# PEER experts: 16 more tokens take gathered rows instead of dense columns, and half the low parts are made on GpSimd

## What is computed

```
sc, pos = lax.top_k(cand, PEER_TOPK)
idx = jnp.take_along_axis(cidx, pos, axis=-1)
gate = jax.nn.softmax(sc, axis=-1)
ug = jnp.take(u_tab, idx, axis=0)
act = jax.nn.gelu(jnp.einsum('td,thkd->thk', xb, ug).astype(jnp.float32), approximate=False)
vg = jnp.take(v_tab, idx, axis=0)
return jnp.einsum('thk,thkd->td', (gate * act).astype(xb.dtype), vg)
```

## Time and profile before

| | us |
|---|---|
| three runs | 3080.49, 3080.64, 3084.59 |
| median | 3080.64 |
| profiled execution, its own time as its span | 3083.4 |
| first stage, first matmul to start of the second | 608.4 to 1303.4 |
| second stage | 1303.4 to 1840 |

### The profile page before, as it was taken

One profiled execution on the slowest core, in us unless ns is written; L12 is line 12 of the kernel. 1 busy time (PEld: TensorE's weight loads), 2 busy tenths in 40 slices (PEclk: granted clock), 3 DMA queues, 4 the chain that ended last, 5 costly groups with the idle time before them and its releaser, 6 DMA issues. The chain is left out here.

```text
span 3083.4 us, 55647 instructions
## 1 busy us (share of the span) xinstructions
PE 3001.1 (97%) x20151; PEld 2650.7 (86%) x20151; DVE 2225.1 (72%) x3952; ACT 981.6 (32%) x1828; POOL 1124.6 (36%) x806
## 2 busy tenths in 40 slices
PE   9999989899999999999999999999999999899999
PEld 7688868799999999999999997768888878688887
DVE  8766687798898898688888887677775345577741
ACT  3444430334433334333333333561111023321110
POOL 4234235222122222243333334214555443345553
PEclk9999999999999999999999999999999999899999
DMA  4000032377877878899999953112223241123233
GB/s 171 28 3 3 3 113 78 131 241 254 299 247 263 286 251 268 297 388 359 352 348 340 354 202 105 33 55 89 96 99 92 79 99 35 58 88 99 98 92 93
DMA packets 242033, 507.91 MB, mean 165 GB/s; under 512 B 44566, under 2 KB 135846, under 8 KB 238412
## 3 DMA queue, kind: packets, MB, share of 16 engines
q1 hardware_dynamic: 183116, 321.11, 31.0%
q0 software_dynamic: 36864, 134.23, 13.4%
q10 hardware_dynamic: 21888, 50.34, 4.2%
HBM read 453.17 MB, written 52.44 MB: 164 GB/s over the span
## 5 line engine op out<-in xcount | busy, mean ns | idle before, releaser
L202 POOL TENSOR_TENSOR up_low<-normed,up_high 128x1024 fp32r<-128x1024 f32 (+1 forms) x136 | 317.0, 2331 | 299.9 <-DVE up_high L197 299.9
L3147 POOL DMA_INDIRECT ev_rows<-in_v,ev_list x128 | 177.3, 1385 | 326.5 <-DVE ev_row_sum L3214 313.6
L207 PE MATMUL up_ps<-ffn_high,up_high 128*128 128x512 f32 x704 | 274.9, 390 | 3.0 <-DVEq L833 3.0
L209 PE MATMUL up_ps<-ffn_high,up_low 128*128 128x512 f32 x704 | 273.9, 389 | 0.0
L208 PE MATMUL up_ps<-ffn_low,up_high 128*128 128x512 f32 x704 | 273.9, 389 | 0.0
L207 PE MATMUL eu_ps<-norm_unit_high,expert_high 128*128 128x384 f32 x768 | 265.7, 346 | 0.0
L209 PE MATMUL eu_ps<-norm_unit_high,expert_low 128*128 128x384 f32 x768 | 258.2, 336 | 0.0
L208 PE MATMUL eu_ps<-norm_unit_low,expert_high 128*128 128x384 f32 x768 | 257.9, 336 | 0.0
L197 DVE CAST up_high<-normed 128x1024 fp32r<-128x1024 f32 (+1 forms) x136 | 92.5, 680 | 205.4 <-PE up_down_ps L209 150.6
L2823 POOL DMA_INDIRECT expert_scores<-in_u,eu_list x64 | 84.0, 1313 | 268.3 <-DVE eu_dots L2851 260.0
L3172 ACT ACTIVATE expert_high<-mixed 128x1024 fp32r<-128x1024 f32 x95 | 100.8, 1061 | 229.3 <-PE ev_acc L209 212.9
(11 more groups left out here) (721 smaller groups left out, 8633.5 us busy)
## 6 DMA issues: line engine op xcount, KB each, us to landing
mixed<-in_v SPq DMA_DIRECT2D x128, 512.0 KB
normed<-in_u SPq DMA_DIRECT2D x125, 512.0 KB
normed<-in_w_up SPq DMA_DIRECT2D x88, 512.0 KB, 3.4
expert_act<-mixed ACTq DMA_DIRECT2D x128, 192.0 KB
expert_gates<-eu_gates ACTq DMA_DIRECT2D x24, 1024.0 KB
expert_scores<-expert_gates SPq DMA_DIRECT2D x16, 1536.0 KB
normed<-expert_act SPq DMA_DIRECT2D x128, 192.0 KB
normed<-in_w_down SPq DMA_DIRECT2D x32, 448.0 KB, 3.3
```

What stands on the lines that cost most here:

```text
L202: return nc.gpsimd.tensor_tensor(low.bitcast(F32R), of, high, ALU.subtract)
L207: nc.tensor.matmul(out, w_high.bitcast(F32R), x_high.bitcast(F32R), start=start, stop=False)
L209: return nc.tensor.matmul(out, w_low.bitcast(F32R), x_high.bitcast(F32R), start=False, stop=stop)
L3147: nc.gpsimd.indirect_dma_start(rows[:, b % 4, :], None, v, bass.IndirectOffsetOnAxis(ap=list_[:, b % 8:b % 8 + 1], axis=0)).then_inc(fetch ...
```

## The change

1. `DENSE` goes from 384 to 368. The last 16 tokens of group 3 take gathered rows too. Their 16 x 128 experts are spread over the 128 partitions, 8 partitions to a token and 16 columns each, so that one gather serves 8 experts of each of the 16 tokens: 16 gathers from each table. Their numbers and gates get into that form through HBM, by two small stores and two loads on SP after tile 33.
2. Group 3 is now chosen first, then 1 and 2. The gate phase of the first round is written out, without the gate matmuls of 2 of its 16 tiles.
3. First stage: VectorE makes only the first half of each low part. For the second half ScalarE copies the PSUM bank once more into SBUF (two places, `copied`), and GpSimd subtracts. GpSimd's program per tile is the low part of tile b+3, then the gather of tile b+3, and from tile 32 on, in every even tile, one more gather (`fetch_more`) into one place, `more.row`: 16 from `u_tab` for the 16 tokens, then 32 from `v_tab` for group 0. VectorE meets it in the odd tile (`meet_more`): a dot, or a weighed sum into `more.sum`.
4. Second stage: 96 + 16 adds instead of 128, in seven of every eight tiles, with seven row places instead of four. At the end eight small matmuls (`together`) sum up the 16 tokens' partitions.
5. The place for all this is the residual `c.x`. It is stored to HBM (2 MB) at the start of `peer_scores` on SP, and loaded again at the end of the second stage.
6. In the memory stage ScalarE spreads the 16 tokens over 128 columns, TensorE turns them by 8 transposes ahead of the first key product, and ScalarE copies the result; the value products wait for that. Semaphores are also cleared at the start of the first stage, on GpSimd.

The core of the diff:

```diff
-DENSE = S - P
+MORE = 16
+SHARE = P // MORE
+DENSE = S - P - MORE
+GROUP_ORDER = (3, 1, 2)
+ROWS_AHEAD = 2 * MORE
+ROW_PLACES = 7
...
                 ahead.load(sp)
+                residual.store(sp)
...
                 nc.scalar.preload_act_table_set("natural_log_exp_and_others")
+                nc.scalar.activation(more.spread.rearrange("p (k t g) -> p k t g", t=MORE, g=SHARE),
+                                     c.h[:, :, S - MORE:S].unsqueeze(3).to_broadcast([P, DT, MORE, SHARE]), ACT.Copy).then_inc(spread_made, 1)
...
+                pe.wait_ge(spread_made, 1)
+                for g in range(2):
+                    for k in range(4):
+                        mm = nc.tensor.transpose(turned_more[g][:, k, :], more.spread[:, (4 * g + k) * P:(4 * g + k + 1) * P], c.ident[:, :])
+                    mm.then_inc(more_turned, 1)
                 key(0)
...
+                def fetch_more(e):
...
+                    pool.wait_ge(more_done, e + 1)
...
+                    of, column = (u, more.list_[:, e:e + 1]) if e < MORE else (v, topk.idx[:, e - MORE:e - MORE + 1])
+                    nc.gpsimd.indirect_dma_start(more.row, None, of, bass.IndirectOffsetOnAxis(ap=column, axis=0)).then_inc(more_fetched, 16)
+
+                def make_low(b):
+                    pool.wait_ge(copy_made, b + 1 + 1)
+                    pool.sem_inc(copy_met, 1)
+                    take_low(nc, low[b % SLOTS][:, 4:8, :], copied[:, b % 2, :].rearrange("p (k n) -> p k n", n=P), high[b % SLOTS][:, 4:8, :]).then_inc(copy_low_made, 1)
...
+                for b in range(KEYS):
+                    if b + ahead < KEYS:
+                        make_low(b + ahead)
+                        fetch(b + ahead)
+                    if b >= FIRST_MORE and b % 2 == 0:
+                        fetch_more((b - FIRST_MORE) // 2)
...
+                def meet_more(i, b):
+                    e = i * (BODY // 2) + (b - FIRST_MORE) // 2
+                    dve.wait_ge(more_fetched, e * 16 + 16)
...
                     make_low(i, b + ahead)
                     dot(i, b)
+                    if b >= FIRST_MORE and b % 2:
+                        meet_more(i, b)
...
+                    act.wait_ge(copy_low_made, i * BODY + b + 1)
+                    nc.scalar.activation(copied[:, b % 2, :].rearrange("p (k n) -> p k n", n=P), ps_u[1][:, :, :], ACT.Copy).then_inc(copy_made, 1)
...
-                        pe.wait_ge(low_made, i * (2 * BODY) + 2 * b + n + 1)
+                        pe.wait_ge(copy_made if n else low_made, i * BODY + b + 1)
...
-                    pe.wait_ge(low_made, i * (2 * BODY) + 2 * b + 2 + 2)
+                    pe.wait_ge(low_made, i * BODY + b + 1 + 1)
+                    pe.wait_ge(copy_low_made, i * BODY + b + 1 + 2)
...
-                        add_row(i, b)
+                        if b in at:
+                            add_row(i, at.index(b))
...
+                sp.wait_ge(row_zeroed, 3)
+                residual.load(sp)
```

More of the change, by code:

```diff
@@ L2126, with peer_scores @@
 WQ_SLOTS = 4
-def peer_scores(nc, c, weights, late, keys_t, scores, topk, ahead):
+def peer_scores(nc, c, weights, late, keys_t, scores, topk, ahead, residual):
     slots = WQ_SLOTS
@@ L2409, with first_choice_and_memory @@
 G_TILES = 16
-def first_choice_and_memory(nc, c, a, topk, h_n, table, ahead):
+FIRST_MORE = U_TILES + BODY
+def first_choice_and_memory(nc, c, a, topk, h_n, table, ahead, more):
     with ExitStack() as ctx:
@@ L2731, in experts_first, with tiles_before, groups_before, stores_before @@
     groups = G_TILES * per_tile
+    whole = MORE // (per_tile * group)
+    chunks = [len(range(n, DENSE // CHUNK, 2)) for n in range(2)]
     ahead = SLOTS - 1
+    def tiles_before(q):
+        return q * G_TILES - (whole if q else 0)
+    def groups_before(q):
+        return q * groups - (whole * per_tile if q else 0)
+    def stores_before(q, n):
+        return q * groups // 8 - (1 if q and n else 0)
     assert rest + BODY == KEYS and groups * group == P and U_TILES == topk.PAUSES
@@ L2793, in _, with loads @@
                     table.load(sp, 0, b + 2)
-                with sp.Fori(1, KEYS // BODY - 1) as i:
-                    for b in range(BODY):
-                        sp.wait_ge(u_turned, i * (2 * BODY) + 2 * b + 2 + 4)
-                        table.load(sp, i, b + 2)
+                def loads(first, last):
+                    with sp.Fori(first, last) as i:
+                        for b in range(BODY):
+                            sp.wait_ge(u_turned, i * (2 * BODY) + 2 * b + 2 + 4)
+                            table.load(sp, i, b + 2)
+                loads(1, 4)
+                sp.wait_ge(chosen, 1)
+                more.store(sp, topk.gate, more_stored)
+                sp.wait_ge(more_stored, 32)
+                more.load(sp, more_listed)
+                loads(4, KEYS // BODY - 1)
                 for b in range(BODY - 2):
@@ L3057, in _, with experts_second @@
                     products(0, b)
-def experts_second(nc, c, v, act_d, second, idx, dots, gate, following, first):
+def experts_second(nc, c, v, act_d, second, idx, dots, gate, following, first, residual, more):
     ahead = SLOTS - 1
@@ L3255, in products @@
                     for k in range(DT):
[L3256 removed]
+                        mm = three_passes(nc, acc[k][:, P:P + DENSE], high[s][:, k, :], low[s][:, k, :], w_high[s][:, :], w_low[s][:, :], start=start, stop=last)
                         if last:
@@ L4645, in experts @@
         stream.early = {b: tuple(x[0][:, b * half:(b + 1) * half, :].rearrange("p k n -> p (k n)") for x in (second.high, second.low)) for b in range(2)}
-        experts_second(nc, c, a["v"], act_d, second, idx, dots, gate[:, 0, :], stream, 4)
+        experts_second(nc, c, a["v"], act_d, second, idx, dots, gate[:, 0, :], stream, 4, residual, more)
     return stream
```

323 lines of the change are left out of this document (204 added, 119 removed).

## The result

The changed kernel takes 3156.07 us (median of 4 runs, 3148.38 to 3159.12) where the kernel before takes 3080.63 (median of 4 on the same chip). The ratio is 1.0239, 95% interval 1.0227 to 1.0251: 75 us slower, where 3052 was forecast and 3036 to 3070 given as the range. The profiled execution spans 3157.4 us.

| stretch, us | before | after |
|---|---|---|
| up to the first stage | 608.4 | 606.0 |
| first stage | 695.0 | 788.4 |
| second stage | 534.5 | 517.3 |
| all behind it | 1245.5 | 1245.7 |

What follows compares the result with a forecast made beforehand. TensorE was taken to set the time from 608 to 1840 us. Terms -41.0 - 1.9 + 1 + 0.9 + 2.5 + 1 + 8 were summed as -27.5; 3083.4 - 27.5 - 2.8 = 3053, given as 3052, range 3036 to 3070.

Steps and rivals of the forecast that it cites:

- The columns: Both stages' matmuls: 16 columns fewer save 0.16 us a tile, -41.0 us in all, ends 0 and 44.
- the slope: TensorE's matmul time per column, 0.417 ns, from spacings of 173.3 ns at 384 columns and 226.7 at 512.
- the rival in which nothing stalls: Both stages: all bounds at their low ends, -42 us, 3039; chance 0.14.
- The memory stage: Ahead of the first stage: ScalarE's spread and TensorE's eight transposes precede the first key, +2.5 us, bounds 0 and 3.1.
- The residual's store: SP's queue ahead of key and weight loads: 2 MB, about 6 us of queue, costs 0, other end 3.
- The start of the first stage: GpSimd clears semaphores and makes lows before it gathers: +1 us, ends 0 and 2.
- the +0.9 of the sum: Second stage's end: eight further small matmuls cost about as much as a last-tile transpose's spreading of matmuls, +0.9 us.
- The step that failed: First stage, single row place: the extra gather leads VectorE's use by 7.3 us in top-k phases, 8.8 in gate phases.
- The price of a late row: First stage: 0.1 us for each of 24 top-k rows, 0.3 for 20 gate rows: +8, upper end 25.
- The slack: VectorE's spare time in the first stage: 1.0 us a pair in a top-k phase, 1.8 in a gate phase.
- The low part on GpSimd: First stage: VectorE loses one low, 0.685 us a tile; GpSimd needs 2.7 of 4.9 us a tile.
- the slower rival: First stage: VectorE stands at the one place, locks and a row's wait of 2.24 us adding up: 3142, chance 0.06.

Runs made afterwards that it cites:

- the run with two places: The changed kernel with a second place for the extra row and each extra gather issued one pair of tiles earlier: 3062.1 us.
- the spaced one: The changed kernel with two row places and 32 first-stage extra rows instead of 48, none beside the wide top-k sums, 16 left to the second stage: 3052.9 us.

## Why the prediction was wrong

**Right.** The columns: a second-stage tile went from 4.16 to 4.00 us, a top-k tile without a stall from 5.04 to 4.87, which is the 0.16 of the slope; the weight load is not the floor, and 0.16 us over 24 matmuls of 16 columns is 0.42 ns a column. The two spacings that the Trainium skill gives ("TensorE: Matmul & The Clock Gate", "Back-to-back issue gap"), 81 ns at 128 columns and 131 at 512, make an estimate of 0.13 ns a column, which is not what this stream does. Without extra rows the time is 3042.7 against 3039 for the rival in which nothing stalls. The memory stage grew by 2.6 us (from 39.7 to 42.3, first transposes to the first stage's), forecast 2.5. The residual's store showed no cost: the memory stage began 3.6 us earlier than before. The start of the first stage did not grow (9.5 us before, 8.1 after, part of it at another clock), forecast +1. The second stage's last tile took 6.8 us instead of 5.2, 0.8 more than the +0.9 of the sum and the shorter matmuls give: the eight small matmuls are two instructions each. The terms of the sum add up to -29.5, not to the -27.5 that I wrote, which makes it 3051 instead of 3053; that is not what failed.

**The step that failed** is this one: "The gather goes out in an even tile behind that tile's low and gather, and VectorE wants it at the end of the odd one, about one and a half tiles later: 7.3 us in a top-k phase, 8.8 in a gate phase." I counted what GpSimd does ahead of the gather (1.27 + 0.94 us) and not what it waits for. Its low part needs ScalarE's copy, which needs the tile's transposes and, in a gate phase, stands behind two gate evictions; GpSimd waited 220.4 + 71.8 = 292 us for it over 126 low parts of the first stage, 2.3 each (its groups from 606 to 1392 us):

```profile
L202 POOL TENSOR_TENSOR expert_low<-residual,expert_high 128x512 fp32r<-128x512 f32 x94 | 163.8, 1743 | 220.6 <-ACT residual L3071 220.4
...
L202 POOL TENSOR_TENSOR norm_unit_low<-residual,norm_unit_high 128x512 fp32r<-128x512 f32 x32 | 50.4, 1575 | 71.8 <-ACT residual L3071 71.8
```

So the issue came 5 to 8 us into the even tile or slid into the odd one, and VectorE had finished the work ahead of the meeting 4.0 us later by the median, where the row lands 6.6 us after its issue. The landing, which I had put at 7.5, was no longer than that; the lead was far shorter. A row's wait of 0 to 2.24 us became 3.5 on average in 35 of 48 meetings, with 7.1 at most.

**The price of a late row** was the second error of size. I let it cost 0.1 to 1.0 us a pair because VectorE had slack, 8 us in all with 25 as the upper end. Against the run without extra rows the first stage lost 788.4 - 673.0 = 115 us: 76 of TensorE standing (83.5 against 7.3) and 39 of longer matmuls (704.9 against 665.7). In the three stretches shown above 382.4 us stand against 306.3 of the run without extra rows, 76 more, and they split into two parts: TensorE's idle time grew by 47 us (50.4 against 3.3), and its busy time for the same matmuls by 29 (332.0 against 303.0), since the clock that is granted behind such a wait is at times the lower one (1.2 instead of 2.4 GHz). The sum had no term for that second part. For the start of the second stage it had +1 with 4 as the upper end, put down to seven gathers at once; TensorE's wait there grew by 7.6 us, and its first tile by 2.3, for the late rows of the first stage.

**The slack** was read from an average. 1.0 us a pair in a top-k phase is true of the whole phase; in its second half, beside the 2048-wide sums, there is none, and a meeting there costs time even if the row is early: about 4 us in each of two top-k phases between the run with two places and the spaced one.

**The low part on GpSimd** stood in the sum as 0.685 us less on VectorE per tile. VectorE's busy time did not fall at all (581 against 579 us): the exclusion of 0.95 us that I had read the earlier trace rows takes back what the move gives. I used it for the slower rival and, in a gate phase alone, set 1.7 us a pair against the slack; the sum had no term for it. By itself it cost no time here (3042.70 against 3042.71 us).

**The rival that came true** was the slower one, VectorE standing at the one place, 3142 us at 0.06. Its place and its chain were right. Its price came near (2.2 to 2.3 us a pair; measured (116.9 - 94.5)/8 = 2.8 in the last gate phase and (149.5 - 117.3)/12 = 2.7 in the last top-k phase), but by other terms and so by luck: it added locks to the wait, where the runs show the wait and the lower clock behind it. Locks were not the reason: with the locks in place and the row met a tile later, 86 us came back. What I held against it ("a VectorE that waits holds no lock") spoke to the locks and not to the lead; the lead should have been followed through every engine, and then its chance would have been more than half.

## What to carry to other kernels

When a transfer has a single place, its lead is the time from when its issuer truly reaches it to when its reader wants it: add up the waits of everything ahead of it on the issuing engine, not only their durations, and compare with the landing time in the trace. If the lead is short, move the issue ahead of work that waits for others, or the reader a tile later; neither added work here. Before work moves from VectorE to GpSimd, look at what GpSimd's operation does to VectorE's operations beside it: here 128 subtractions with two SBUF inputs left VectorE as busy as before.

## What the runs showed of the hardware

A GpSimd subtraction of 128x512 from two SBUF inputs lengthens VectorE's two-input operations by as much as it saves there: 1.54 instead of 0.69 us for a one-hot build, 1.37 instead of 1.21 for a dot on average, 2.58 for one behind a wide sum. VectorE's low part, which reads PSUM and SBUF, kept its 0.69 us beside it (0.68 in the 26 that overlap one, in the run without extra rows). It isn't two-input operations alone: of the 16 copies of 128x8 (`expert_dots`) in that stage the 12 that overlap a GpSimd low part take 1.0 to 1.1 us and end with it, the 4 others take 0.17, while the top-k's MAX8 operations of 128x256 take 0.40 to 0.41 either way. And waits of 3 to 5 us of TensorE cost more than their length: behind the wait of 3.21 us eight transposes took 1.87 us instead of 1.04, and the stretches with such waits show a granted clock of 0.91 instead of 1.00.
